# Down weights of a mixture-of-experts layer: the same four transfers, cut by partitions instead of by chunks

## The chip, the cores and the metric

The kernel runs on one core of a Trainium2 chip. The core has five engines that run their own instruction streams and meet at semaphores: TensorE (PE, matrix products), VectorE (DVE), ScalarE (ACT), GpSimd (POOL) and SyncE (SP), which here only issues transfers. Sixteen DMA engines move data between the chip's main memory (HBM) and the on-chip memory of 128 partitions. The metric is the device time of one execution in microseconds, as a median over runs.

## The reference

One layer of a streaming encoder over 2048 tokens of width 1024, all in float32. A norm and an input projection feed two groups of heads: stick-breaking attention (8 heads of 64) and an RWKV-7 recurrence (8 heads of 64). Their outputs go through an output projection and are added to the input. Then comes the part that matters here, a mixture of 32 experts in four groups: each token takes the best group, and in it the best two experts.

```
h2    = rms_norm(x, norm2_gain)
group = argmax(h2 @ w_rg)                    # 4 groups
top_p, top_i = top_k(softmax(logits of the group's 8 experts), 2)
gates = group_prob * top_p / sum(top_p)
# each expert e on its tokens, w_g[e], w_u[e]: (1024, 512), w_d[e]: (512, 1024)
out_e = (silu(xb @ w_g[e]) * (xb @ w_u[e])) @ w_d[e]
x     = x + sum over the token's two experts of gate * out_e
```

An expert has 2 MB each of gate, up and down weights. All 32 are read once, 192 MB.

## The kernel before, in words

The program runs in stages: projection of the tokens and attention, the recurrence, the output projection with the routing (`mix_out_and_route`), the placing of tokens in a table of blocks (`place_slots`), and the experts (`run_experts`). The experts' stage begins about 2.1 ms into the span.

**Blocks.** A block is up to 32 tokens of one expert. There are 144 blocks in this run, three to five for most experts. A block's rows are held as 128 partitions by 256: partition group q (32 partitions, `QUARTERS`) holds the q-th quarter of the width of its 32 tokens. TensorE does three groups of products per block: gate (`gate_ps`, L2246), up (`up_ps`, L2246) and down (`y_ps`, L2260). It runs a step ahead: gate and up of block b+1 come before down of block b.

**Order around a block.** VectorE turns the gathered rows of the next block (`xT`, L2318), forms the hidden product (`h`, L2332), turns it (`hT`, L2336) and writes the row numbers for the scatter (`put`, L2323). ScalarE computes the silu (L2303) and copies the result out (`y`, L2297). GpSimd gathers rows by an indirect DMA (`xg`, L2207) and adds results into the output by another (`out`, L2215). There are two buffers of `xg`, `y`, `put` and `take`, used in turn. VectorE's write of `put` for block b waits until the scatter of block b-2 has landed (`stored`), and the next block's work stands behind it on VectorE. On GpSimd the gather that waits for the hidden product of a block stands ahead of the scatter of the block before it.

**Weights.** `ExpertWeights` has three slots. Experts 0 and 1 are loaded in the routing stage, one third of an expert per pair of tiles (L1797); the loads stand in SyncE's one queue among the loads and stores of the tiles. Expert 2 is loaded as the experts' stage begins. From then on SyncE loads expert e+3 into the slot of expert e as soon as the last down product of e is done (`refill`). An expert's load is four gate transfers and four up transfers (L1683) and four down transfers (L1687), each of 512 KB, in this order. TensorE waits once per expert, ahead of its first gate product, for all twelve (`weights_of`).

In on-chip memory the down weights have the shape 128 x 4 x 1024: partition q*32+p, chunk k holds row q*128 + k*32 + p of the expert's 512 rows. This order makes 32 rows of one chunk and quarter the counterpart of a 32-partition group of `hT`.

Of the kernel before, what the change touches and what calls it, by code (L numbers as in the profile page):

```python
# [24 lines left out]
P = 128  # L25
# [12 lines left out]
FF = 512  # L38
ROWS = 32
# [93 lines left out]
def project_tokens(nc, ctx, program, front, x, norm1_gain, w_in, sb_q_gain, sb_k_gain, qT_dram, kT_dram, v_dram):  # L133
# [44 lines left out]
    def on_sync(sp, first_weights):  # L178
# [3 lines left out]
        def store(t, s):  # L182
# [3 lines left out]
            sp.dma_start(v_dram[bass.ds(t * P + 1, P), :], qkv[:, s, 2, :]).then_inc(stored, 16)  # L186

        load(0, 0)
        with nc.allow_non_contiguous_dma("a small vector, once"):
            sp.dma_start(gain[:, :], norm1_gain[0, :].rearrange("(k p) -> p k", p=P)).then_inc(gains, 16)  # L190
        sp.dma_start(qk_gain[:, 0, :], sb_q_gain[0, :].partition_broadcast(P)).then_inc(gains, 16)
        sp.dma_start(qk_gain[:, 1, :], sb_k_gain[0, :].partition_broadcast(P)).then_inc(gains, 16)
        for part in range(3):
            cols = slice(part * SBW, (part + 1) * SBW)
            sp.dma_start(w_sb[:, :, cols], w_in[0, :, cols].rearrange("(k p) c -> p k c", p=P)).then_inc(w_loaded[part], 16)
            if part == 0:
                load(1, 1)
# [3 lines left out]
        with sp.Fori(0, NT // 2 - 1) as i:  # L201
            for s in range(2):
                t = i * 2 + s
                sp.wait_ge(x_turned, t + 1)
                load(t + 2, s)
                store(t, s)
# [1445 lines left out]
class ExpertWeights:  # L1652
# [20 lines left out]
    def load(self, sp, turn, s, part=None):  # L1673

        w_g, w_u, w_d = self.dram
        e = turn % N_GROUPS * PER_GROUP + turn // N_GROUPS
        for x, (to, src) in enumerate(((self.wg, w_g), (self.wu, w_u))):
            if part in (None, x):  # L1680
                rows = src[0, bass.ds(e, 1), :, :].rearrange("o (p k) f -> p (o k) f", p=P)
                for k in range(0, KT, 2):
                    sp.dma_start(to[s][:, k:k + 2, :], rows[:, k:k + 2, :]).then_inc(self.gu_loaded[s], 16)  # L1683
        if part in (None, 2):
            rows = w_d[0, bass.ds(e, 1), :, :].rearrange("o (q k p) d -> (o q) k p d", q=4, k=FF // P)
            for k in range(FF // P):
                sp.dma_start(self.wd[s][:, k, :], rows[:, k, :, :]).then_inc(self.d_loaded[s], 16)  # L1687


class MixOut:  # L1690
# [714 lines left out]
```

## Time and profile before

| | us |
|---|---|
| runs of the kernel before (three) | 3346.57, 3359.8, 3365.17 |
| their median | 3359.8 |
| the profiled execution's own time | 3338.16 |
| its span, first to last instruction | 3336.4 |
| TensorE busy in the span | 2729.9 (82%) |
| VectorE, ScalarE, GpSimd busy | 1227.2, 880.6, 805.3 |

The profile is of one execution. Its slices cut the span into forty equal parts and give a digit per part for the busy share of an engine, the granted clock of TensorE and the mean busy share of the sixteen DMA engines. Such a mean does not say whether all sixteen are busy for part of the time or some of them for all of it. The share of a short window can come out a little over 1, since packets overlap. The list of waits puts each idle stretch of an engine down to what released it; where the trace names nothing it says "issue". In the timeline each row has the start, how long it took, and the engine, line, operation, output and inputs; SyncE's rows there (SPq) are the issue of transfers, and an issue that takes long was held back by the transfers ahead of it.

### The profile page before, as it was taken

What the parts mean: (1) busy time and instruction counts of PE and PEld (TensorE: products, weight loads), DVE (VectorE), ACT (ScalarE), POOL (GpSimd) and SP (SyncE); (2) the same over time, 40 slices, a digit from 0 to 9 for tenths busy, and PEclk for the clock granted to TensorE, in tenths of its full rate; (3) what the DMA queues carried; (4) which work ended last, traced back from release to release, by engine and by line L of the source; (5) the groups of instructions that cost most, each with busy time, mean ns of one, the idle gap of its engine ahead of it and who ended that gap; (6) DMA issues with size and microseconds to landing.
All of it is one profiled execution on the core that took longest, in us unless ns stands there. A gap on an engine that the chain in (4) does not pass through costs nothing. (4 is left out here: it accounts for less than half of the span.)

```text
span 3336.4 us, 103696 instructions
## 1 busy us (share of the span) xinstructions
PE 2729.9 (82%) x45126; PEld 1859.5 (56%) x45127; DVE 1227.2 (37%) x2580; ACT 880.6 (26%) x1768; POOL 805.3 (24%) x815
## 2 busy tenths in 40 slices
PE   8999999999999968888889886866566776656657
PEld 4444444446666657777764444655455565545545
DVE  2333211128878856666643335211111111111111
ACT  1121100016666655555533333100000000000000
POOL 0000300001101055656520001332222333223323
PEclk9999999999999989999999897988788888878878
DMA  4122311112220201111105431677666666656663
GB/s 129 51 63 63 105 57 57 57 46 65 61 64 14 80 28 40 38 44 39 46 15 189 171 131 62 193 190 194 190 197 186 187 186 187 188 181 198 192 191 76
DMA packets 207148, 371.28 MB, mean 111 GB/s; under 512 B 33697, under 2 KB 133537, under 8 KB 204162
## 3 DMA queue, kind: packets, MB, share of 16 engines
q1 hardware_dynamic: 179106, 328.72, 30.0%
q0 software_dynamic: 27744, 38.03, 6.3%
q8 instruction: 255, 4.18, 0.5%
q14 instruction: 43, 0.35, 0.0%
HBM read 296.17 MB, written 70.52 MB: 110 GB/s over the span
## 5 line engine op out<-in xcount | busy, mean ns | idle before, releaser
L2246 PE MATMUL gate_ps<-wg_,xT 128*32 128x128 f32 x6336 | 223.7, 301 | 286.2 <-DMA wd_<-in_w_exp_down 268.8
L2246 PEld LDWEIGHTS gate_ps<-wg_,xT 128*32 128x32 f32 x6336 | 197.3, 122 | 321.2 <-issue 277.9
L712 DVE TENSOR_TENSOR_SCAN h_all<-h_all 128x512 f32<-128x512 f32 (+3 forms) x320 | 345.8, 1129 | 69.0 <-ACT h_all L664 42.9
L2207 POOL DMA_INDIRECT xg<-h,take x146 | 144.2, 988 | 815.5 <-DVE h L2332 677.5
L344 PE MATMUL ps<-low,high 128*128 128x512 f32 x768 | 337.6, 596 | 2.5 <-issue 2.5
L2260 PE MATMUL y_ps<-wd_,hT 128*32 128x256 f32 x4608 | 274.4, 379 | 0.6 <-ACT y L2297 0.6
L1713 PE MATMUL ps<-high 128*128 128x512 f32 x512 | 236.5, 613 | 34.1 <-DMA high<-mixT 33.9
L2318 DVE STREAM_TRANSPOSE xT<-xg 128x256 f32<-128x256 f32 x145 | 64.6, 445 | 534.1 <-PE up_ps L2246 503.6
L2215 POOL DMA_INDIRECT out<-y,put x144 | 228.8, 1589 | 56.4 <-issue 51.9
L344 PEld LDWEIGHTS ps<-low,high 128*128 128x128 f32 x768 | 144.6, 192 | 173.4 <-issue 173.4
L2303 ACT ACTIVATE sil<-gate_ps 128x128 f32<-128x128 f32 x144 | 40.0, 278 | 644.4 <-PE gate_ps L2246 644.4
L690 POOL TENSOR_SCALAR_AFFINE_SELECT h_all<-h_all 128x256 f32<-128x256 f32 x64 | 39.7, 620 | 703.6 <-ACT h_all L664 703.4
L2246 PE MATMUL gate_ps<-high,xT 128*32 128x128 f32 x2880 | 102.5, 303 | 124.1 <-DMA wd_<-in_w_exp_down 96.8
L2246 PE MATMUL up_ps<-wu_,xT 128*32 128x128 f32 x6336 | 200.4, 281 | 0.0
L444 PE MATMUL ps<-h_all,w_first 128*128 128x512 f32 x448 | 193.6, 592 | 0.0
L2260 PEld LDWEIGHTS y_ps<-wd_,hT 128*32 128x32 f32 x4608 | 142.1, 110 | 79.1 <-ACT y L2297 1.1
L2246 PEld LDWEIGHTS up_ps<-wu_,xT 128*32 128x32 f32 x6336 | 184.5, 115 | 1.5
L664 ACT ACTIVATE h_all<-ps 128x1024 f32<-128x1024 f32 (+3 forms) x160 | 143.7, 899 | 151.6 <-PE ps L617 151.5
L2297 ACT COPY y<-y_ps 128x256 f32<-128x256 f32 x144 | 53.7, 373 | 482.5 <-PE y_ps L2260 467.2
L1713 PEld LDWEIGHTS ps<-high 128*128 128x128 f32 x512 | 97.1, 196 | 143.5 <-issue 142.7
L628 PEld LDWEIGHTS ps<-ident,h_all 128*128 128x128 f32 x1088 | 116.0, 141 | 106.9 <-DVE h_all L712 76.6
L2323 DVE COPY put<-to_all 128x1 int32 (+1 forms) x144 | 20.7, 144 | 410.4 <-DMA out<-y,put 410.4
(318 smaller groups left out, 4717.1 us busy)
## 6 DMA issues: line engine op xcount, KB each, us to landing
wd_<-in_w_exp_down SPq DMA_DIRECT2D x128, 512.0 KB
wg_<-in_w_exp_gate SPq DMA_DIRECT2D x88, 512.0 KB
wu_<-in_w_exp_up SPq DMA_DIRECT2D x88, 512.0 KB
high<-in_w_exp_gate SPq DMA_DIRECT2D x40, 512.0 KB
high<-in_w_exp_up SPq DMA_DIRECT2D x40, 512.0 KB
pT<-low SPq DMA_DIRECT2D x13, 1024.0 KB, 3.9
rkv<-pT SPq DMA_DIRECT2D x96, 128.0 KB, 2.5
high<-in_x SPq DMA_DIRECT2D x16, 512.0 KB, 4.0
```

Source lines behind the costliest of these rows:

```text
L344: done = pe.matmul(qkv_ps[:, part, :], hT[:, s, k, :], w_sb[:, k, part * SBW:(part + 1) * SBW], start=(k == 0), stop=(k == KT - 1))
L444: last = pe.matmul(p_ps[:, s, g, :], w[s][:, k, :], h_all[:, k, g * GT:(g + 1) * GT], start=(k == 0), stop=(k == KT - 1))
L628: last = pe.transpose(prodT_ps[h][:, b * P:(b + 1) * P], prod[:, n % KEPT, h, b * P:(b + 1) * P], ident[:, :])
L664: act.activation(keep[:, n % KEPT, :, 0:w], z_ps[n % 2][:, :, 0:w], ACT.Sigmoid, scale=-SCALE).then_inc(kept, 1)
L712: dve.tensor_tensor_scan(prod[:, n % KEPT, h, 0:w][:, ::-1], rows, rows, so_far, ALU.mult, ALU.bypass).then_inc(scanned, 1)
L1713: done = pe.matmul(self.ps[:, s, half, :], self.rows[:, s, k, :], self.w[:, k, half * 512:(half + 1) * 512], start=(k == 0), stop=(k == KT ...
L2207: pool.indirect_dma_start(out=xg[j][:, :], out_offset=None, in_=h2_quarters[:, :], in_offset=bass.IndirectOffsetOnAxis(ap=take[j][:, 0:1], ...
L2215: pool.indirect_dma_start(out=out_quarters[:, :], out_offset=bass.IndirectOffsetOnAxis(ap=put[j][:, 0:1], axis=0), in_=y[j][:, :], in_offs ...
L2246: last = pe.matmul(to_ps[QUARTERS[q], 0:P], xT[:, k * ROWS:(k + 1) * ROWS], w[:, k, q * P:(q + 1) * P], start=(k == 0), stop=(k == KT - 1))
L2260: last = pe.matmul(y_ps[QUARTERS[q], 0:256], hT[:, k * ROWS:(k + 1) * ROWS], wd[s][:, k, q * 256:(q + 1) * 256], start=(k == 0), stop=(k = ...
L2297: act.copy(y[j][:, :], y_ps[:, 0:256]).then_inc(y_copied, 1)
L2318: dve.transpose(xT[:, :], xg[j][:, :])
```

## The change

The four transfers of an expert's down weights are cut in another way. Before, transfer k moves chunk k of all 128 partitions; its source is walked as (4, 32, 1024), quarter, row and column. Now, transfer q moves all four chunks of the 32 partitions of quarter q; source and destination are both walked as (32, 4, 1024). Rows, places, bytes (512 KB each), the number of transfers, their place in SyncE's queue and the semaphore's counts are the same; every contiguous run is a row of 4 KB in both. The order of the instructions on all engines is unchanged; in SyncE's stream the twelve-transfer loads differ in the shape of the last four, `128x1x1024` before and `32x4x1024` now.

```
         if part in (None, 2):
-            rows = w_d[0, bass.ds(e, 1), :, :].rearrange("o (q k p) d -> (o q) k p d", q=4, k=FF // P)
-            for k in range(FF // P):
-                sp.dma_start(self.wd[s][:, k, :], rows[:, k, :, :]).then_inc(self.d_loaded[s], 16)
+            rows = w_d[0, bass.ds(e, 1), :, :].rearrange("o (q k p) d -> q p (o k) d", q=4, k=FF // P)
+            for q in range(4):
+                sp.dma_start(self.wd[s][q * ROWS:(q + 1) * ROWS, :, :], rows[q]).then_inc(self.d_loaded[s], 16)
```

`ROWS` is 32.

## Rows read from the trace of the kernel before

**Rows 1.** Slices of the span: DMA engines' mean busy share (tenths), rate moved.
```profile
DMA  4122311112220201111105431677666666656663
GB/s 129 51 63 63 105 57 57 57 46 65 61 64 14 80 28 40 38 44 39 46 15 189 171 131 62 193 190 194 190 197 186 187 186 187 188 181 198 192 191 76
```

**Rows 2.** Waits, whole span: who for whom; us in total, times, longest us.
```profile
DVE put L2323 <- DMA out<-y,put: 410.4, 110, 6.5
...
PE gate_ps L2246 <- DMA wd_<-in_w_exp_down: 365.6, 26, 21.3
...
PE ps L1713 <- DMA high<-mixT: 33.9, 3, 13.6
...
PE gate_ps L2246 <- issue: 22.6, 2, 12.5
```

**Rows 3.** Windows: length; busy PE, PEld, DVE, ACT, POOL; PEclk; DMA share; GB/s.
```profile
2101.18:3317.54 1216.36, 817.29 (x22849) 687.59 (x22853) 185.74 (x856) 102.45 (x355) 365.11 (x284) 0.83 0.63 185
2704.00:2706.00 2.00, 2.00 (x48) 1.84 (x43) 0.00 (x0) 0.00 (x0) 0.00 (x0) 0.50 0.25 78
...
2728.00:2730.00 2.00, 2.00 (x82) 2.00 (x76) 0.00 (x0) 0.28 (x1) 1.18 (x2) 1.00 1.03 367
...
18.00:20.00 2.00, 2.00 (x3) 0.67 (x2) 0.92 (x2) 0.41 (x3) 0.00 (x0) 1.00 1.04 386
```

**Rows 4.** Timeline of SyncE's queue, 2695 to 2740 us: start, us, what.
```profile
2697.37 20.78 SPq L1687 DMA_DIRECT2D wd_<-in_w_exp_down  x4
2719.74 9.19 SPq L1683 DMA_DIRECT2D wg_<-in_w_exp_gate  x4
2729.02 9.39 SPq L1683 DMA_DIRECT2D wu_<-in_w_exp_up  x4
```

**Rows 5.** DMA view, 2300 to 3200 us: packets, MB, share of sixteen engines; scatters.
```profile
q1 hardware_dynamic: 37742, 141.39, 46.1%
q0 software_dynamic: 19620, 26.85, 16.3%
...
out<-y,put POOLq DMA_INDIRECT x102
```

**Rows 6.** Timeline of TensorE, first gate products after a wait.
```profile
2742.85 3.64 PE L2246 MATMUL gate_ps<-high,xT 128*32 128x128 f32 x64 [10.06 <-issue]
...
2750.84 1.92 PE L2246 MATMUL gate_ps<-high,xT 128*32 128x128 f32 x64
...
2756.05 1.92 PE L2246 MATMUL gate_ps<-high,xT 128*32 128x128 f32 x64
```

**Rows 7.** Timeline of GpSimd and VectorE, 2705 to 2760 us.
```profile
2717.07 1.59 POOL L2215 DMA_INDIRECT out<-y,put  x1 [0.39 <-issue]
...
2725.66 0.15 DVE L2323 COPY put<-to_all 128x1 int32 x1 [4.34 <-DMA out<-y,put]
...
2726.98 0.34 DVE L2332 SCALAR_TENSOR_TENSOR h<-sil,gate,up_ps 128x128 f32<-128x128 f32 x1
...
2728.11 0.99 POOL L2207 DMA_INDIRECT xg<-h,take  x1 [3.81 <-DVE h L2332]
...
2729.80 1.59 POOL L2215 DMA_INDIRECT out<-y,put  x1 [0.71 <-issue]
```

**Rows 8.** Windows, each from a scatter's last issue to VectorE's next `put`.
```profile
2753.97:2759.77 5.80, 5.80 (x185) 4.96 (x181) 1.05 (x4) 0.80 (x3) 2.58 (x2) 1.00 0.47 132
2731.39:2738.56 7.17, 1.40 (x28) 0.58 (x20) 1.05 (x4) 0.52 (x2) 2.58 (x3) 0.74 1.00 326
2284.77:2293.14 8.37, 7.02 (x196) 5.26 (x188) 1.32 (x7) 0.89 (x4) 2.58 (x2) 1.00 1.00 245
```

**Rows 9.** Timeline of SyncE's queue, 1796 to 1870 us, routing stage.
```profile
1817.20 0.34 SPq L1779 DMA_DIRECT2D out<-x_t  x1
...
1821.43 6.18 SPq L1687 DMA_DIRECT2D wd_<-in_w_exp_down  x4
...
1834.04 11.07 SPq L1779 DMA_DIRECT2D out<-x_t  x1
...
1866.67 0.34 SPq L1779 DMA_DIRECT2D out<-x_t  x1
```

## The prediction, made before the changed kernel had run

> **What bounds the kernel now.** I began with the slices of the whole span. In the last third the core moves about 190 GB/s, three times what it moves in most of the attention and recurrence stages, and the DMA engines' mean busy share is only 0.6 to 0.7 [rows 1]. A mean of 0.65 can be sixteen engines with pauses, or a few that never pause beside many that idle. The waits say that the transfers matter: TensorE sat idle 365.6 us in 26 waits ahead of an expert's first gate product until the down weights had landed, and 22.6 us in two more that the trace puts down to nothing, 388 us in all [rows 2]. The long waits of VectorE for the scatters (410.4 us) are in the same list and cost little so far; they come back below.
>
> Then I asked which engines are busy. While only down weights are in flight the share stands at 0.25 and the rate at 78 GB/s; when the gate and up weights run it is 1.03 at 367 GB/s, and the load of the input projection at the program's start reaches 386 GB/s at 1.04 [rows 3]. A quarter of sixteen is four: a down transfer, whose source has four as its first index, is carried by four engines of about 20 GB/s each. SyncE's queue shows the same from its side. Issuing four down transfers takes it 20.78 us of back-pressure, four gate or up ones of the same size 9.2 and 9.4 us [rows 4]. So 2.1 MB of an expert's 6.3 MB sits on four engines, which set the pace for all: per expert they carry 0.52 + 0.26 MB, the other twelve 0.26 MB. Over 900 us of this stage the direct queue moved 141.39 MB [rows 5], which is 22.5 experts at 6.29 MB, or 40.0 us per expert. Thirty of 32 experts load within the stage or at its edge, the first two earlier.
>
> From the first gate product (2101.18) to the last block's (3317.54) is 1216.4 us [rows 3]. There are 144 blocks, so 143 steps between them. An undisturbed step is 5.21 us [rows 6], which would make 745 us. [...]
>
> **The change.** No instruction is added, removed or moved on any engine. An expert still has four down transfers of 512 KB, in packets of one 4 KB row, into the same places. What changes is the shape of each: 32 partitions by four rows, both sides with 32 as the first index. I expect sixteen engines on each. [...]
>
> Step 1, the engines' time. In the 900 us, the direct queue's packets took 46.1% of sixteen engines for 22.5 experts: 0.461 x 900 / 22.5 = 18.4 us per expert, if spread evenly. The gathers and scatters took 16.3% for 102 blocks, 1.44 us per block, 6.5 us for the 4.5 blocks of a mean expert [rows 5]. Sum 24.9 us, against 40.0 us now. TensorE needs at least 4.5 x 5.21 = 23.4 us. So the transfers stop being the bound by far, but they only just fit.
>
> Step 2, what is late next. The stall goes, and the engines will be nearly full while TensorE works; now they are full mostly while it waits. What suffers is the scatter of a block's result. VectorE may rewrite the row numbers of a buffer only when the scatter of two blocks before has landed, and stands in line with that wait ahead of the next block's transpose and hidden product, which release TensorE and the next gather. The loop is in [rows 7]: scatter issued 2717.07, 1.59 us on GpSimd, 7.00 us until VectorE goes on at 2725.66, hidden product done at 2727.32 (1.66 later), gather starts 0.79 later and takes 0.99, next scatter of this buffer pair 0.70 later at 2729.80. That is 5.73 us plus the landing time L, for two blocks: 12.73 us, or 6.37 per block. L depends on the load: 5.80 us at a share of 0.47, 7.17 us at 1.00, 8.37 us at 1.00 with only 245 GB/s [rows 8]. With the engines busy 24.9 of some 28 us I take L = 6.8, between the first two and nearer the full one: a step of (5.73 + 6.8) / 2 = 6.27 us. Times 143 that is 896 us in place of 1216.4: 320 us less. Bounds: 5.21 us per step if neither scatter nor transfer ever holds (745 us, 471 less); L = 8.37 throughout gives 7.05 us, 1008 us, 208 less. [...]
>
> Step 3, the stage before. The down weights of the first two experts are loaded between the tiles of the output projection. The store of a tile comes every 16.84 us, but 32.63 us lie between those around such a load (1834.04 to 1866.67), whose issue took 6.18 us and whose successors waited in the queue behind it [rows 9]. That is 15.8 us, twice; TensorE's own idle time for the mixed rows is 33.9 us in three waits [rows 2]. Gate and up parts, of the same 2.1 MB, sit there too without a wait of this length in that list. I take 30 us off; bounds are 0 and 34. It hides nothing else: the routing that follows needs every tile. A third such load, at the start of the expert stage, is for a slot that is read only after the experts of the other two slots; I take nothing for it.
>
> **The sum.** Span 3336.4, execution 3338.2 us. 3338.2 - 320 - 30 = 2988 us. The median of the runs before, 3359.8, is 0.6% above this execution, whose time lies under the lowest run's 3346.6; by the same ratio 2988 would be 3007. I predict 3000 us.
>
> [...] Sixteen engines in one transfer of 32 partitions could be held on the side where they write. The trace has no large transfer into 32 partitions, so from rows alone its rate is bounded by 78 GB/s (four engines, no gain) and 367 GB/s (full). [...]
>
> **Rivals.**
>
> *A cap at half rate on the new shape.* [...] Half of 386 GB/s is 193: 2.1 MB then takes 10.9 us instead of 5.4, 5.5 more per expert, so 30.4 us per expert, more than the 28.2 of my forecast. The transfers stay the bound, but the 28 waits shrink: 28 x (40.0 - 30.4) = 269 us less, with 30 before it 3039 us by the profiled execution, some 3050 as a median. For it: each group's rows lie close together. Against it: four engines bring 78 GB/s or more between them today, 20 each, although all four write at once, and queued transfers may overlap on different groups.
>
> *The scatters don't suffer.* L stays 5.80, since a third of the direct packets only move from four queues to sixteen and none gets the long backlog. Step (5.73 + 5.80) / 2 = 5.77, 825 us, 391 less: 2917, as a median about 2930. Against it is that all 30 loads would have to fall as today in TensorE's pauses, which are gone.
>
> *Nothing changes.* The engine count does not follow the shape. Then the four-engine share of 0.25 stays, and the time stays at 3340 to 3365. The contrast of 0.25 and 1.03 between shapes of equal size speaks against it.
>
> *Slower.* The loop of step 2 is the one place where wider transfers can cost more than the waits that they end: each scatter packet now finds weight packets queued on every engine, not on four. The loss decides once 143 steps exceed 1216 + 30 us, a step of 8.71 us, which is L = 2 x 8.71 - 5.73 = 11.7 us. At L = 13 it would be 9.37 us a step, 1339 us, and 3338 + 123 - 30 = 3431 us. For it: L did grow by 1.4 to 2.6 us from a half to a full load. Against it: the largest L shown is 8.37.
>
> **How the numbers follow.** Forecast 0.50; cap at half rate 0.25; scatters unhurt 0.18; nothing changes 0.03; slower 0.03; anything else 0.01. The forecast's own bounds as medians are about 2930 (L = 5.80) and, with L = 8.37, 3338 - 208 - 30 = 3100, near 3115. Both large rivals lie between 2930 and 3050. To leave out two in ten I take 2900 to 3085. No change is within 0.5%, 17 us, about what a measurement of this kernel can tell: faster 0.95, same 0.02, slower 0.03.
>
> **What would show it.** The share of 0.25 must vanish and the stage run at 250 GB/s or more. Step 1: SyncE's issue of four down transfers falls from some 20 to under 10 us; TensorE's waits for down weights fall from 366 to under 40 us. Step 2: most steps between gate products 5.8 to 6.6 us, and more waits of TensorE for the hidden product. Step 3: all stores 17 us apart. If 26 waits of 3 to 8 us remain instead, the cap is there; if the steps are 5.3 to 5.8, L did not grow. A span above 3100 us would make the whole account wrong.

## The result, and the profile after

The changed kernel takes 3164.1 us (median of three runs, 3162.66 to 3166.12) against 3359.8 us. The ratio is 0.9425, with a 95% interval of 0.9382 to 0.9469. The forecast was 3000 us, 2900 to 3085: the direction was right, the size was not. Of 360 us forecast, 196 came. By single executions, the forecast's own sum was 2988 us and the profiled one took 3164.1, 176 us more.

The slices [rows 1] show the experts' stage moving more per second than before, though still not all the time:

```profile
DMA  3212221112102201111110555148787787788882
GB/s 124 67 56 60 86 81 60 60 48 85 58 15 64 90 12 30 42 41 41 39 52 12 168 170 175 73 129 253 201 246 218 207 236 208 213 254 216 230 237 40
```

The waits, as who for whom, us in total, times, longest, answer [rows 2]. The line on the down weights is gone. The wait for the mixed rows has lost 22 us, VectorE's wait for scatters 93. What is new is the last line: TensorE was idle 318 times ahead of gate products, and the trace knows no releaser for it ("issue"); before it was 2 times. TensorE's waits for the hidden product, which the prediction expected to grow, are 17 as before, 10.6 us in all.

```profile
PE ps L1713 <- DMA high<-mixT: 11.8, 3, 7.6
...
DVE put L2323 <- DMA out<-y,put: 317.2, 93, 6.4
...
PE gate_ps L2246 <- issue: 141.8, 318, 8.1
```

SyncE's queue, start and us, answers [rows 4]. The four down transfers are issued in 2 us, like the others; it was 20.78.

```profile
2595.14 2.14 SPq L1683 DMA_DIRECT2D high<-in_w_exp_gate  x4
2597.39 2.00 SPq L1683 DMA_DIRECT2D high<-in_w_exp_up  x4
2599.48 1.97 SPq L1687 DMA_DIRECT2D wd_<-in_w_exp_down  x4
```

Windows with the columns of [rows 3]: the whole expert stage from its first gate product to the last block's, then pieces of the load just issued. The long stretches at a share of 0.25 are gone: of the stage's windows of 2 us, 103 of 608 had a share of 0.235 to 0.275 before, up to four in a row, and 10 of 530 have it now, none beside another. But within one load the gate and up weights arrive at up to 420 GB/s, and the down weights, which come last in it, at 206 to 225 GB/s in the windows shown, under the same full share. From 2622 to 2624 almost nothing is in flight (a share of 0.05) and TensorE stops.

```profile
2081.50:3141.54 1060.04, 891.04 (x22848) 742.06 (x22852) 183.62 (x856) 102.41 (x355) 364.99 (x284) 0.97 0.77 213
2604.00:2606.00 2.00, 1.70 (x61) 1.52 (x59) 0.31 (x2) 0.28 (x1) 0.64 (x1) 1.00 1.03 420
...
2614.00:2616.00 2.00, 2.00 (x58) 1.96 (x53) 0.97 (x4) 0.39 (x2) 0.54 (x1) 1.00 1.06 225
2616.00:2618.00 2.00, 1.44 (x31) 0.66 (x20) 0.00 (x0) 0.13 (x1) 1.62 (x2) 1.00 0.99 206
2622.00:2624.00 2.00, 0.36 (x7) 0.00 (x0) 1.14 (x6) 0.37 (x1) 0.30 (x1) 1.00 0.05 9
...
3114.00:3116.00 2.00, 1.92 (x51) 1.21 (x44) 0.41 (x3) 0.37 (x1) 1.28 (x2) 1.00 0.04 8
```

TensorE's timeline (start, us, what, how many, idle time ahead) answers [rows 6]. The 64 gate products of a block break up into 39, 3, 5 and 17 with pauses of about 0.3 us: from 2601.37 to the first up product at 2604.94 they take 3.57 us, where [rows 6] has one piece. (Two rows can overlap, since the ends of products are modelled.) The third block shown stands at 3116.38, near the stage's end, where the share is 0.04, so no weights are in the way there. And 2626.04 is the first block of another pass of the loop over experts: TensorE was idle for 3.68 us before it, for no reason that the trace can name.

```profile
2601.37 1.40 PE L2246 MATMUL gate_ps<-wg_,xT 128*32 128x128 f32 x39
2603.01 0.42 PE L2246 MATMUL gate_ps<-wg_,xT 128*32 128x128 f32 x3 [0.24 <-issue]
2603.75 0.43 PE L2246 MATMUL gate_ps<-wg_,xT 128*32 128x128 f32 x5 [0.32 <-issue]
2604.47 0.71 PE L2246 MATMUL gate_ps<-wg_,xT 128*32 128x128 f32 x17 [0.30 <-issue]
2604.94 1.99 PE L2246 MATMUL up_ps<-wu_,xT 128*32 128x128 f32 x64
...
2626.04 2.58 PE L2246 MATMUL gate_ps<-wg_,xT 128*32 128x128 f32 x64 [3.68 <-issue]
...
3116.38 0.43 PE L2246 MATMUL gate_ps<-wg_,xT 128*32 128x128 f32 x6 [0.33 <-issue]
```

### The profile page after: what moved, and what is told of

Read it like the earlier page. It is cut to its first block and busy times, and to the rows that moved or that the text cites. A ratio compares the mean times of both kernels' runs of the same rounds, so it can differ in the third digit from the quotient of the medians.

```text
span 3162.3 us, 103696 instructions
## 1 busy us (share of the span) xinstructions
PE 2806.8 (89%) x45126; PEld 1917.4 (61%) x45127; DVE 1227.6 (39%) x2580; ACT 880.5 (28%) x1768; POOL 803.8 (25%) x815
## 5 line engine op out<-in xcount | busy, mean ns | idle before, releaser
L2246 PE MATMUL gate_ps<-wg_,xT 128*32 128x128 f32 x6336 | 291.9, 289 | 134.0 <-issue 113.7
L2246 PEld LDWEIGHTS gate_ps<-wg_,xT 128*32 128x32 f32 x6336 | 213.2, 116 | 211.8 <-issue 184.3
L2260 PE MATMUL y_ps<-wd_,hT 128*32 128x256 f32 x4608 | 296.5, 380 | 5.0 <-issue 4.5
L2260 PEld LDWEIGHTS y_ps<-wd_,hT 128*32 128x32 f32 x4608 | 213.7, 110 | 33.2 <-issue 5.2
L2246 PE MATMUL up_ps<-wu_,xT 128*32 128x128 f32 x6336 | 212.7, 277 | 2.9 <-issue 2.6
L2246 PEld LDWEIGHTS up_ps<-wu_,xT 128*32 128x32 f32 x6336 | 192.9, 112 | 7.5 <-issue 7.0
L444 PE MATMUL ps<-h_all,low 128*128 128x512 f32 x384 | 165.8, 592 | 0.0
L628 PE MATMUL ps<-ident,h_all 128*128 128x128 f32 x1088 | 155.1, 281 | 4.5 <-DVE h_all L712 4.1
```

What stands on the lines that cost most here:

```text
L444: last = pe.matmul(p_ps[:, s, g, :], w[s][:, k, :], h_all[:, k, g * GT:(g + 1) * GT], start=(k == 0), stop=(k == KT - 1))
L628: last = pe.transpose(prodT_ps[h][:, b * P:(b + 1) * P], prod[:, n % KEPT, h, b * P:(b + 1) * P], ident[:, :])
L2246: last = pe.matmul(to_ps[QUARTERS[q], 0:P], xT[:, k * ROWS:(k + 1) * ROWS], w[:, k, q * P:(q + 1) * P], start=(k == 0), stop=(k == KT - 1))
L2260: last = pe.matmul(y_ps[QUARTERS[q], 0:256], hT[:, k * ROWS:(k + 1) * ROWS], wd[s][:, k, q * 256:(q + 1) * 256], start=(k == 0), stop=(k = ...
```

## The experiments

Four chips were used, here called A to D. Each ratio is to the kernel before on the same chip. A step is the time from one block's first gate product to the next block's. "Stage" is the time from the first gate product to the last block's, 143 steps, in the one execution that was profiled; before it was 1216.4 us in [rows 3], after it is 1060.0 us.

**The two kernels again.** e1 and e9 are the changed kernel and e2 the kernel before, none edited; e1 and e2 ran on one chip, e9 on another.

> The changed kernel once more, unchanged. Its first trace has a gate product of 3.4 us in nearly every block, against 1.75 us before, with idle stretches of 0.3 us inside it that the trace puts down to issue. Theory A (the slow gate product belongs to the changed program, wherever it is loaded): again 3.3 to 3.6 us, time within 0.5% of 3164 us. Theory B (it is a matter of one loading of the program, not of the change): the gate product is 1.75 us here, and the time falls to 2930 to 2990 us.

> The kernel before once more, unchanged. Theory A: gate product 1.75 us in blocks that no load holds up, ratio to the kernel before 0.995 to 1.005. Theory B: it may come out with a gate product of 3.4 us in this loading; it would cost little here, since the loads of 40 us per expert bound it: ratio 1.00 to 1.02.

> The changed kernel a third time, for comparison with the others of this group. So far the gate product's length goes with the chip: 3.4 us on the one where the kernel before ran at a mean clock of 0.94, 1.75 us where it ran at 0.92, in all runs of either. [...]

| kernel, chip | median us | ratio (95%) | stage | median gate product | median step |
|---|---|---|---|---|---|
| e1 after, chip A | 3156.25 | 0.9403 (0.9375-0.9430) | 1059.2 | 3.38 | 6.97 |
| e2 before, chip A | 3360.98 | 1.0002 (0.9978-1.0027) | 1228.0 | 3.40 | 6.94 |
| e9 after, chip C | 3097.08 | 0.9271 (0.9223-0.9319) | 1003.7 | 1.76 | 6.33 |

The slow gate product does not come from the change. On chip A the kernel before has it too. This is e2's timeline of TensorE, after a wait for down weights: the first block's gate product is whole, the second's falls into the same pieces.

```profile
2913.86 3.64 PE L2246 MATMUL gate_ps<-wg_,xT 128*32 128x128 f32 x64 [13.55 <-DMA wd_<-in_w_exp_down]
...
2921.21 1.27 PE L2246 MATMUL gate_ps<-wg_,xT 128*32 128x128 f32 x40
2922.83 0.39 PE L2246 MATMUL gate_ps<-wg_,xT 128*32 128x128 f32 x2 [0.35 <-issue]
2923.53 0.42 PE L2246 MATMUL gate_ps<-wg_,xT 128*32 128x128 f32 x5 [0.31 <-issue]
2924.26 0.71 PE L2246 MATMUL gate_ps<-wg_,xT 128*32 128x128 f32 x17 [0.30 <-issue]
```

It hardly showed in the kernel before, since the loads paced it at 40 us per expert: its median was 3359.66 on chip A and 3339.81, 3343.78 and 3348.41 on three others. Once the loads no longer pace it, 1.65 us per block count: the changed kernel is 59 us slower on A than on C. The kernel before had a mean granted clock of 0.938 to 0.943 in all its 23 executions on A, and of 0.914 to 0.921 in all 29 on the three others; the trace that the forecast rested on has 0.917 and the fast gate product, and its own 3338.16 us lies under all three runs of the table before. The runs of the result have 0.965 to 0.970, near e1 (0.970 to 0.973) and not e9 (0.951 to 0.954). By these signs the forecast was read from a trace of one kind and measured on the other. What sets the kinds apart was not found. Each chip was used at one time only, so it may be the chip or something else that held for all its runs.

**TensorE's loops.** The program on TensorE is a loop over groups of three experts with, inside, a loop over an expert's blocks. e6 writes the outer loop out; e5 writes out both, with this input's numbers of blocks as constants; e8 is e5 with the down loads of before; e7 is e6 with the inner loop turned, so that its branch stands ahead of the down product. All ran on chip B, whose gate product is not slow (1.75 us at the median in e6). They ask whether TensorE's idle stretches with no releaser in the trace go with the branches of its loops.

```
e6 -  with pe.Fori(0, (NE - 1) // SLOTS) as i:
   -      for x in range(SLOTS): one_expert(i * SLOTS + x + 1, ...)
   +  for e in range(1, NE): one_expert(e, e % SLOTS, e // SLOTS)
e5 +  counts = (5, 4, 5, 4, ..., 4, 5, 5)
   +  for e, count in enumerate(counts):
   +      weights_of(e % SLOTS, e // SLOTS)
   +      for n in range(count): gate_up(...); down(...)
e7    (e6 and)  gate_up(start + 1, s)
   +  with pe.Fori(1, count - 1) as n: down(...); gate_up(start + n + 1, s)
   +  down(start + count, s, ahead=2)
```

> The changed kernel with TensorE's part of the expert stage written out: no loop and no branch, the blocks per expert as constants of this input (5, 4, 5, 4, 4, ...). [...] Rival S (the slow gate product is TensorE's or the chip's own at these products): gate products stay at 3.4 us, time within 1% of the changed kernel.

> The changed kernel with only the outer loop over experts written out; the loop over an expert's blocks stays. [...]

> As the one with the outer loop written out, and the inner loop turned: the same order of products, but the branch stands ahead of the down products, not of the gate products. TensorE uses up the down products' instructions at half the pace (32 in 1.75 us against 64). [...] Rival S: no difference to the one with the outer loop written out.

> The kernel before, with TensorE's part of the expert stage written out as in the first of these. [...]

e6: 3063.51 us, ratio 0.9184 (0.9130 to 0.9238), stage 959.7. e5: 3159.16 us, 0.9470 (0.9418 to 0.9522), stage 1053.0. e7: 3090.62, 0.9259 (0.9209 to 0.9309). e8: 3336.52, 1.0000 (0.9971 to 1.0029). TensorE's waits over the stage, first of e9, then of e6 (in which the hidden product's line has another number):

```profile
PE gate_ps L2246 <- DVE h L2332: 113.4, 49, 5.8
...
PE gate_ps L2246 <- issue: 70.5, 9, 9.1
```

```profile
PE gate_ps L2246 <- DVE h L2329: 127.4, 58, 5.5
PE y_ps L2260 <- issue: 20.6, 6, 5.2
...
PE gate_ps L2246 <- issue: 0.9, 2, 0.7
```

Nine waits for nothing, one ahead of the first block of each pass of the outer loop after the first, are gone, and 44 us of the stage with them (the two ran on different chips of the same kind; e10 and e11 below differ by the same edit on one chip, and by 55 us). So with the loads of the change the branch back over some 2,000 instructions (three experts with two written-out blocks of 320 each) goes with 44 to 55 us; what TensorE waits for there, the trace does not name. In the kernel before, writing the loops out gained nothing (e8, ratio 1.0000; e13 below, with one more edit, 0.9955), since TensorE stands still for weights there anyway.

Straight code is not free of such waits either. With the loads of the change, e5 takes 96 us more than e6. The waits of e5, then two windows and its timeline around one of them:

```profile
PE gate_ps L2246 <- issue: 106.8, 40, 5.5
PE up_ps L2246 <- issue: 62.7, 37, 4.8
PE y_ps L2260 <- issue: 45.8, 15, 4.8
```

```profile
2406.00:2408.00 2.00, 0.00 (x0) 0.00 (x0) 0.00 (x0) 0.00 (x0) 1.59 (x1) 1.00 1.07 229
2408.00:2410.00 2.00, 0.00 (x0) 0.00 (x0) 0.00 (x0) 0.00 (x0) 0.00 (x0) 0.64 1.06 256
```

```profile
2404.43 1.04 PE L2246 MATMUL gate_ps<-wg_,xT 128*32 128x128 f32 x29
2410.94 2.13 PE L2246 MATMUL gate_ps<-wg_,xT 128*32 128x128 f32 x34 [5.46 <-issue]
```

TensorE stops for 5.46 us in the middle of 64 products that need nothing new, while the DMA engines are full. Such waits sum to 215 us over the stage. The same straight code in e8, with the down weights on four engines, has next to none inside a block:

```profile
PE up_ps L2246 <- issue: 6.5, 6, 2.1
...
PE y_ps L2260 <- issue: 3.2, 4, 1.1
```

So of these two runs straight code waited in the one whose loads kept all sixteen engines full. e5 carried 134 instruction packets in 800 us (2200 to 3000 us), with 1.1% of the sixteen engines' time, the changed kernel 71, with 0.6%. Whether those packets were late, and TensorE with them, no row shows. e7 moves a branch behind which nothing is slow on this chip (gate products of 1.75 us in e6), and it was not run on chip A. That it lost 27 us against e6 stays unexplained: in the profiled executions 15 us of it lie ahead of the experts' stage, where the two programs are the same (first gate product at 2094.07 against 2078.77), and 17 in it.

**The write side.** e3 splits the four down transfers into sixteen of 128 KB and alternates the groups of partitions (the semaphore's counts, not shown, follow). e4 gives every partition whole rows of its own, so that each transfer covers 128 partitions, and pays with a moving operand of gate and up products that steps by four elements; only the order of the sums in the result changes. e14 leaves the down weights and splits the gate weights by 32 partitions, with the same packets in the same places. The three ask whether the down weights' rate comes from the side that is written, 32 partitions at a time, or from the side that is read.

```
e3  +  for k in range(FF // P):
    +      for q in (0, 2, 1, 3):
    +          sp.dma_start(self.wd[s][q*ROWS:(q+1)*ROWS, k, :], rows[q, :, k, :])
e4  +  rows = w_d[...].rearrange("o (p k) d -> p (o k) d", k=FF // P)
    +      sp.dma_start(self.wd[s][:, k, :], rows[:, k, :])
    +  ... w[:, k, q * P:(q + 1) * P].rearrange("p (c k) -> p k c", k=FT)
e14 +  for g in (4 groups of 32 partitions if x == 0 else all 128):
    +      for k in range(0, KT, 2):
    +          sp.dma_start(to[s][g, k:k + 2, :], rows[g, k:k + 2, :])
```

> The down weights in sixteen transfers of 128 KB, one per chunk and quarter, quarters in the order 0, 2, 1, 3. [...] Rival Q (the down rows are slow to read, whatever is written): it stays at 210 to 225 GB/s. [...]

> The down weights in four transfers of all 128 partitions, each partition's rows beside each other in memory; the gate and up products take their weight columns with a step of four, so that the hidden columns stand in the matching order. The result is the same sum in another order. [...] What the step of four costs TensorE no row shows: bounds are 0 and a doubling of gate and up products (1.75 us to 3.5 us each, 500 us in all). Where it costs nothing and the gate product is 1.75 us, 2930 to 2960 us; with the slow gate product 3100 to 3170 us.

> The changed kernel, but the gate weights too are moved by groups of 32 partitions, group after group, in sixteen transfers of 128 KB with the same 4 KB packets; they are read in the same order of memory as any 32 partitions of the transfers before. Theory P (32 neighbouring partitions are written at half rate): while only gate weights move the rate falls from 385 to 415 GB/s to 205 to 230 GB/s. Rival Q (the down weights' rows are slow to read): the gate phase stays above 350 GB/s.

e3 (chip A): 3140.39 us, 0.9344 (0.9317 to 0.9372), stage 1043.9. e4 (chip A): 3471.31 us, 1.0326 (1.0295 to 1.0356). e14 (chip D): 3094.59 us, 0.9258 (0.9222 to 0.9295), stage 992.4. e14's queue and windows over one load, in the order gate, up, down:

```profile
2367.39 8.79 SPq L1685 DMA_DIRECT2D high<-in_w_exp_gate  x16
2376.28 2.74 SPq L1685 DMA_DIRECT2D high<-in_w_exp_up  x4
2379.11 1.81 SPq L1689 DMA_DIRECT2D wd_<-in_w_exp_down  x4
```

```profile
2372.00:2374.00 2.00, 2.00 (x79) 1.94 (x74) 0.11 (x1) 0.28 (x1) 0.00 (x0) 1.00 1.03 199
...
2388.00:2390.00 2.00, 0.00 (x0) 0.00 (x0) 0.86 (x4) 0.00 (x0) 0.65 (x1) 1.00 1.13 354
...
2392.00:2394.00 2.00, 1.72 (x34) 1.60 (x38) 0.10 (x1) 0.00 (x0) 0.24 (x1) 0.50 1.00 201
```

Here the gate weights come at 199 GB/s into 32 partitions at a time; the up weights behind them, unchanged, at 354; the down weights at 201. Windows also hold the packets of gathers and scatters and vary with them, so here is the rate of the weights alone, over the middle 80% of each third of a load (median of the stage's last 28 loads, worked out from the packets in the traces):

| GB/s | gate | up | down |
|---|---|---|---|
| after | 297 | 365 | 201 |
| e14, gate by groups of 32 partitions | 192 | 311 | 196 |
| e4, down weights into 128 partitions | 292 | 418 | 351 |
| e3, sixteen alternating down transfers | 289 | 365 | 234 |

e4's down weights in one window:

```profile
2404.00:2406.00 2.00, 2.00 (x44) 1.74 (x39) 0.47 (x2) 0.52 (x2) 0.99 (x1) 1.00 1.03 416
```

Both slow kinds of transfer also read one contiguous quarter of their weights, which the fast ones do not. That this is not the cause is shown by the weights of the output projection (L1706): eight transfers in a row, each of one contiguous 512 KB, but into 128 partitions. In the trace after:

```profile
1098.00:1100.00 2.00, 2.00 (x26) 1.71 (x27) 1.76 (x3) 1.55 (x4) 0.64 (x1) 1.00 1.03 416
```

So the low rate goes with writing into 32 partitions at a time: the gate weights fell from 297 GB/s to 192 with it (after and e14), and the down weights rose from 201 to 351 without it (after and e4). How the write side holds them no run shows. e4 itself lost by its other half: a gate or up product group takes some 3.9 us with the stepped operand, and a step 9.1 to 9.7 us. Without it, on the same chip (e1), the up products take about 1.9 us and the gate products 3.4.

```profile
2413.80 4.20 PE L2246 MATMUL gate_ps<-wg_,xT 128*32 128x128 f32 x62
2417.77 3.95 PE L2246 MATMUL up_ps<-wu_,xT 128*32 128x128 f32 x64
```

e14, with a second third of the load at the low rate (192 GB/s), is as fast as e9 (ratios 0.9258 and 0.9271). So load time by itself is not what bounds the changed kernel.

**The scatters.** In e9 an expert's last block falls into the down weights' part of the next load. VectorE, then TensorE:

```profile
2228.84 0.15 DVE L2323 COPY put<-to_all 128x1 int32 x1 [8.40 <-DMA out<-y,put]
```

```profile
2223.38 1.92 PE L2260 MATMUL y_ps<-wd_,hT 128*32 128x256 f32 x32
2230.54 3.45 PE L2246 MATMUL gate_ps<-high,xT 128*32 128x128 f32 x64 [5.25 <-DVE h L2332]
```

Two windows of the same stretch, one in the wait and one over the gate product after it:

```profile
2226.00:2228.00 2.00, 0.00 (x0) 0.00 (x0) 0.00 (x0) 0.00 (x0) 0.00 (x0) 1.00 1.07 249
...
2230.54:2233.99 3.45, 3.45 (x72) 3.22 (x76) 0.59 (x3) 0.00 (x0) 2.40 (x2) 0.55 1.04 404
```

VectorE waits 8.40 us for a landing, TensorE 5.25 us for VectorE, and then TensorE runs its gate product at a granted clock of 0.55, in 3.45 us. The up products right behind it, as many, took 1.92 us at 1.00. e10 moves the rewriting of the row numbers: a buffer's numbers are written one block later, where its scatter has had a block's time more to land. e11 is e10 and e6 together.

```
e10 -  number_rows(b, j, i)
    +  if not first: number_rows(b - 1, 1 - j, i - 1 + j)
    +  (after the last pair) number_rows(last * 2 + 1, 1, last)
```

> The changed kernel, but VectorE writes a block's row numbers (put) one block later, behind the next block's hidden product; so it waits for a scatter 5 us later and nothing stands behind the wait that TensorE needs soon. Theory L (my step 2: under full load the scatters land after 7 to 11 us, and VectorE's wait for them holds TensorE): on a fast chip TensorE's waits for the hidden product vanish and 60 to 130 us go; on a slow chip, where a step takes 6.9 us anyway, the last blocks of an expert fall from some 7.5 us to 6.9 us, 10 to 30 us in all. Rival: the scatters' landing times aren't what the last blocks wait for: no change over 0.3%.

> Outer loop over experts written out, and the late put. Theory L on a fast chip: from 3063 us (outer loop written out alone) to 2900 to 2970 us; steps of 5.2 to 5.6 us. On a slow chip 3050 to 3090 us. Rival: unchanged against the one with the outer loop written out.

e10 (chip C, beside e9): 3013.73 us, 0.9019 (0.8977 to 0.9060), stage 921.2, median step 5.24 in place of 6.33. e11: 2963.88 us, 0.8862 (0.8821 to 0.8903), stage 866.5. Two of e10's waits; in e9 the first was 70.5 us in 9, the second 438.5 us in 107:

```profile
PE gate_ps L2246 <- issue: 100.0, 21, 8.7
DVE put L2323 <- DMA out<-y,put: 53.1, 38, 3.7
```

TensorE's waits for the hidden product fell from 113.4 us to 0.9. Moving the wait took 82 us off the stage. Some of what it freed returned as waits put down to issue, in the first line, which had lain under it.

**All of it, and none of the change.** e12 is e11 with e3's sixteen transfers. e13 is e11 with the down loads of before.

> As the one before, with the down weights in sixteen transfers of 128 KB, quarters in the order 0, 2, 1, 3. [...] Rival Q (slow to read): the same time as the one before. It is the candidate for the best version.

> Outer loop written out and late put, as in a kernel above that ran at 0.886 of the kernel before, but with the down weights as before the change, by chunks on four engines. If those two edits gain by themselves: well below 3343 us. If they only free what the change needs (four engines carry 40 us per expert and hide both): 3310 to 3345 us, ratio 0.99 to 1.00, and the change is worth 11% there against 7% in the kernel as it stands.

e12 (chip C): 2916.37 us, 0.8723 (0.8683 to 0.8763), the fastest of all, stage 823.3 against 745 for 143 undisturbed steps. The sixteen alternating transfers save 47.5 us here (e11 to e12) and saved 16 on chip A (e1 to e3), where the wait for scatters, the outer loop and the slow gate product were all still in the way; which of the three hid the rest was not tested. Windows of the down part of a load in e12 have 225 to 315 GB/s; two of them:

```profile
2414.00:2416.00 2.00, 1.27 (x21) 0.50 (x13) 0.46 (x3) 0.00 (x0) 0.74 (x1) 1.00 1.06 315
2416.00:2418.00 2.00, 0.63 (x5) 0.16 (x5) 0.22 (x1) 0.14 (x1) 0.24 (x1) 1.00 1.04 280
```

e13 (chip D): 3325.26 us, 0.9955 (0.9927 to 0.9984). Without the change the two edits are worth 0.5%, with it 4.4% (e9 to e11). The wait for the ends of the loads hides them, as it hid the slow gate product.

## Why the prediction came out as it did

**Step 1, the engines' time: right.** The stretches at a share of 0.25 and TensorE's 366 us for down weights are gone. The working that gave 24.9 us per expert gives 26.9 on the trace after (2200 to 3000 us): 20.8 us of direct packets and 6.1 of gathers and scatters. The stage takes 33 us per expert, so the transfers are no longer the bound, as forecast.

**The cap: the rival was real, and its time was wrong.** The down weights came at 188 to 212 GB/s, median 201, or 10.4 us per 2.1 MB; the rival had 193 GB/s and 10.9 us. Its factor of a half was an assumption, which no row of the trace before shows; the runs showed 201 GB/s beside the 386 that it halved, a factor of 0.52. The reason held against it, that groups might overlap, came true only in part, and only with the groups alternated in small transfers (234 GB/s in e3). But its 3039 us rested on 28 remaining waits for down weights, and there is none. It acts on something else: the engines stay full longer, while an expert's last blocks scatter (landings of 9.27 us in the down part of e9, below).

**Step 2 failed, and most of all in what it took for granted.** It put the stage at 896 us, and the stage took 1060.0, 164 more. The experiments divide this, one after the other, partly across chips:

- The undisturbed step of 5.21 us was read from one trace and taken as a property of the program. On a chip with the slow gate product the same kernel's stage is 56 us longer (1059.2 or 1060.0 against 1003.7). An undisturbed step there is 5.21 + 1.65 = 6.86 us, above the 6.27 of the forecast, so that neither the scatter nor the load sets the typical step; 143 such steps are 981 us. On such a chip 896 us was out of reach.
- That all 143 steps are alike, an expert's first block among them: 44 us (1003.7 to 959.7), at the nine passes of the outer loop. In the kernel before those blocks waited for weights anyway, which covered it: writing the loops out there (e8) gained nothing.
- The landing time L: most of the remaining 64 us (959.7 to 896; e6 also has 20.6 us of waits put down to issue ahead of down products, which the prediction did not have). The mechanism was right, since moving the wait (e10) took 82 us away, and TensorE's waits for the hidden product fell from 113.4 us to 0.9. The term L was mis-sized and given as one number: over e6's 109 waited landings the median is 7.37 us, the mean 7.73, a tenth lie over 10.29, and the longest is 11.07; the prediction took 6.8, with 8.37 as the bound, from three windows. In the kernel before, all 110 waited landings have a median of 6.29 us and none takes over 8.4, so no row of that trace showed the long ones.

These come to 164. The median step of e6, 6.37 us against 6.27 forecast, is luck. The prediction said that most steps would lie between 5.8 and 6.6 us; 20 of 143 do, 52 take under 5.4, and a tenth over 9.3 (in the profiled execution after, 5 of 143 lie between 5.8 and 6.6). Its formula holds for the average only: with L = 7.73 it gives 6.73 us, and the mean step is 6.71.

L depends on which third of a load is in flight, which three windows could not show. In e9 the waited landings have medians of 6.87 us in the gate part, 6.42 in the up part and 9.27 in the down part (22, 29 and 52 landings, placed by the bytes that the queue had carried). On chip A, the sixteen alternating transfers bring the down part from 9.32 (e1) to 7.48 (e3). So the cap and the scatter, two rivals in the prediction, meet in one stretch. But the low rate alone does not make a landing late: in e14's gate part, at 192 GB/s in transfers of 128 KB, the median is 5.24 us (35 landings), and in its down part, in transfers of 512 KB, 8.62 (42). The two parts differ in the size of the transfers; whether that is what matters, no run isolates.

The clock adds to the last two items of the list: in the row of e9, after 5.25 us of idle time, the gate product took 3.45 us at a granted clock of 0.55, where one at 1.00 takes some 1.9. The forecast's 6.27 us for every step has nothing for it.

**Step 3, the stage before: right in kind, 20 us in place of 30.** The first gate product came at 2081.50 instead of 2101.18. In the profiled executions of e1 and e9 it came at 2071.54 and 2070.45, in the other ones with sixteen engines between 2071.54 and 2094.07; with the loads of before (e2, e8, e13) between 2103.49 and 2110.50. So 30 was within reach, and a single pair of executions does not tell it from 20. The pause of 32.63 us between stores around the first down load [rows 9] became 16.83 us.

**What would show it.** The list was right on the share, SyncE's issue, the stores and the waits for down weights. It was wrong on the steps, on the stage's 250 GB/s (213 moved), and on TensorE's waits for the hidden product: no more than before in the profiled execution after, though 49 in e9. It said that a span over 3100 us would make the whole account wrong, and the span was 3162.3. By the runs, steps 1 and 3 stand and step 2 fell. The slow gate product is not all of it: without it (e9, 3097.08 us) the time still misses the range, by 12 us.

## What to carry to other kernels

When a transfer stops pacing a loop, every small idle time that lay under it counts from then on. Before forecasting the new pace, list what the engine does at each branch and each long wait "for nothing", and ask whether the undisturbed step was measured on more than one chip. Choose the shape of a load by both ends, the engines that it is spread over and the partitions that it writes (here 78 GB/s on four engines, 201 into 32 partitions, 351 into 128), and keep work that waits for a small transfer to land away from a load's slowest part (here landings of 9.27 us against 6.42 and 6.87).

## What the runs showed of the hardware

- TensorE's time for the same products differed between chips (or between the times at which they were used). On chip A a block's 64 gate products take 3.4 us where they take 1.75 on B, C and D, with pauses of 0.3 us after some 40 products, at a granted clock of 1.00 and with nearly idle DMA engines (a share of 0.04). The kernel before has it on A as well. Why was not settled.
- The branch back of a loop of some 2,000 instructions went with waits of 3.6 to 9.1 us that the trace puts down to issue, nine in all (e9); writing the loop out took 44 to 55 us off the stage. Wholly straight code had 215 us of waits under full DMA engines (e5) and, inside the blocks, 10 us with the weights partly on four engines (e8).
- The weights alone came at 188 to 201 GB/s (medians by run) where a transfer writes 32 partitions, and at 289 to 418 where it writes 128. Alternating the groups in transfers of 128 KB gave 234 (e3).
- A moving fp32 operand that steps by four elements made 64 up products of 128 columns take 3.95 us in place of about 1.9 (e4 and e1, one chip).
- The scatters that VectorE waited for landed in 6.4 to 6.9 us at the median under gate and up weights and in 9.3 under down weights, 11.3 at the longest (e9).
